# The token gather of a routed mixture-of-experts stage: one fp32 product, or two single-pass products of a high and a low part

## The chip, the cores and the metric

The kernel runs on one core of one Trainium2 chip. The metric is the device time of one execution in microseconds (us), as a median over repeated runs. The profile used below is that of one further execution.

## What is computed

The reference is a stack of twelve stages over 256 tokens of width 1024 in fp32: an S5 and pooling mixer, a stick-breaking attention, two mixture-of-experts (MoE) feed-forward stages, and a second block of convolution, recurrent and latent-attention mixers with dense feed-forwards. The change touches only the two MoE stages:

```python
def grouped_moe(x, router_w, router_bias, w1, w3, w2):
    xt = x.reshape(-1, d)
    scores = jax.nn.sigmoid((xt @ router_w).astype(F32))
    ...                       # best group of four experts, best two experts in it
    gates = jnp.sum(jax.nn.one_hot(idx, N_EXPERTS, dtype=F32) * w[..., None], axis=1)
    h = jax.nn.silu(jnp.einsum('td,edf->etf', xt, w1)) * jnp.einsum('td,edf->etf', xt, w3)
    h = h * gates.T[:, :, None].astype(h.dtype)
    y = jnp.einsum('etf,efd->td', h, w2)
```

Every token uses one group of four experts only, so the kernel sorts the tokens by group and runs each group's experts on its own tokens.

## The kernel before, in words

**Streams.** All weights come from memory as 840 tiles of 128 x 1024 fp32 values (512 KB), through a ring of six buffers `raw`. For each tile ScalarE (ACT) writes the rounded high part `w_hi` (`split_hi`, L265) and VectorE (DVE) the rest `w_lo = raw - w_hi` (`split_lo`, L272), both of type fp32r, which TensorE (PE) multiplies in a single pass. A weight product is three such products: high x high, low x high, high x low (`three_by_token`, L296 to L298, 512 columns; `three`, L289 to L291, 256 columns). The queue of SyncE issues the loads; a buffer is reloaded when DVE has split it. PE has tile n when DVE has written its `w_lo`.

**An MoE stage.** Its order on each engine is written out by hand. `moe_pe` multiplies the router weights (L758, L759), then the eight tiles of a gate projection (`ple gate`), and inside it `ranks_pe`, which counts how many earlier tokens go to the same group. Meanwhile `route_dve` chooses experts and `slots_dve` turns the choice into a one-hot matrix: `slots[p, tt, s]` (2 x 640 columns) is 1 where token `tt*128 + p` sits in slot s (L938). The largest group has two slot tiles of 128 (the first 256 slots), the three other groups one each (the other 384, `REST`).

**The gather.** `gather_pe` starts when the gate projection ends. It forms the gates by slot (L833, 4 columns), turns the one-hot matrix by ten PE transposes (L841), and then gathers the tokens: `x.T @ slots`, for each 128-wide chunk of the 1024 features over the two token tiles. First the 256 slots of the largest group, two chunks to a PSUM bank, banks `Q[0]` to `Q[3]` (L848, 16 products), then the 384 others, one chunk to a bank, the four banks in turn (L856, 16 products). Operands are plain fp32:

```python
last = nc.tensor.matmul(bank(Q[i])[:, c % 2, :], x[:, tt, c * P:(c + 1) * P], slots[:, tt, 0:T], ...)
last = nc.tensor.matmul(b[:, 0:REST], x[:, tt, k * P:(k + 1) * P], slots[:, tt, T:SLOTS], ...)
```

ACT rounds each filled bank to its high part (L808, L811), DVE subtracts it for the low part (L898, L902) and so frees the bank; `before(pe, Q[i])` makes PE wait for that. In ACT's order (`moe_act`) the three copies of the turned matrix (L803) and two weight tiles (L265) stand ahead of L808, in DVE's order (`moe_dve`) two weight tiles (L272) stand ahead of L898.

**The experts.** `experts_pe` follows at once. The four experts of the largest group pass two token tiles over each weight tile, the other twelve one.

Of the kernel before, what the change touches and what calls it, by code (L numbers as in the profile page):

```python
# [8 lines left out]
F32 = mybir.dt.float32  # L9
# [3 lines left out]
ACT = mybir.ActivationFunctionType  # L13
ALU = mybir.AluOpType
# [3 lines left out]
T = 256  # L18
# [126 lines left out]
def build(nc, dram, columns, stages, known):  # L145
    starts, n_tiles = stream_plan(stages)
    ctx = ExitStack()
    with ctx:
# [63 lines left out]
        def region(at, *shape):  # L212

            size = math.prod(shape)
            ap = scr[:, at:at + size]
            if len(shape) == 2:
                return ap.rearrange("p (a b) -> p a b", b=shape[1])
            if len(shape) == 3:
                return ap.rearrange("p (a b c) -> p a b c", b=shape[1], c=shape[2])
            return ap  # L220

        def column(name, i=0, n=1):
            at = columns[name] + i
            return par[:, at:at + n]
# [4 lines left out]
        def bank(b):  # L229
            return b[:, :].rearrange("p (a t) -> p a t", t=T)  # L230
# [13 lines left out]
        x_first = region(9216, KC, T)  # L244
        ple_tanh = region(6144, TT, D)
        routing = region(8704, 512)
        slots = region(9216, TT, SLOTS)
        slots_turned = c_hi[:, 4:4 + SLOT_TILES + 1, :]

        class Stream:  # L250
# [7 lines left out]
        def split_hi(act, tiles=2):  # L258

            for n in range(act_at.tile, min(act_at.tile + tiles, n_tiles)):  # L260
                act.wait_ge(raw_in[n % RING], 16 * (n // RING + 1))
                if n >= RING:
                    used, count = pe_did.tile(n - RING)
                    act.wait_ge(used, count)
                nc.scalar.activation(w_hi[:, n % RING, :], raw[:, n % RING, :], ACT.Copy).then_inc(hi_done, 1)  # L265
                act_at.tile = n + 1

        def split_lo(dve, tiles=2):

            for n in range(dve_at.tile, min(dve_at.tile + tiles, n_tiles)):  # L270
                dve.wait_ge(hi_done, n + 1)
                nc.vector.tensor_tensor(w_lo[:, n % RING, :], raw[:, n % RING, :],  # L272
                                        w_hi[:, n % RING, :].bitcast(F32), ALU.subtract).then_inc(lo_done, 1)
                dve_at.tile = n + 1
# [509 lines left out]
        def moe_act(act, st):  # L784
            def tanh_of_gate(half):
                for tt in range(TT):
                    act.wait_ge(pe_did["ple gate"], pe_did.at("ple gate", st, half, tt))
                    nc.scalar.activation(ple_tanh[:, tt, half_of(half)], Q[2 * half + tt][:, :], ACT.Tanh, scale=0.5).then_inc(
                        act_did["ple tanh"], act_did.next("ple tanh", st, half, tt))

            split_hi(act)
            split_hi(act)
            act.wait_ge(dve_did["logits"], dve_did.at("logits", st))
            nc.scalar.activation(routing[:, 0:32], routing[:, 480:512], ACT.Tanh, scale=0.5).then_inc(
                act_did["router tanh"], act_did.next("router tanh", st))
            split_hi(act)
            tanh_of_gate(0)
            split_hi(act)
            tanh_of_gate(1)
            for i in range(3):  # L800
                act.wait_ge(pe_did["gathered"], pe_did.at("gathered", st, "turned", i))
                n = min(2, SLOT_TILES - 2 * i)
                nc.scalar.activation(slots_turned[:, 2 * i:2 * i + n, :], bank(Q[1 + i])[:, 0:n, :], ACT.Copy).then_inc(  # L803
                    act_did["xg_hi"], act_did.next("xg_hi", st, "turned", i))
            split_hi(act)
            for i in range(4):
                act.wait_ge(pe_did["gathered"], pe_did.at("gathered", st, i))
                nc.scalar.activation(pair(x_hi, i), bank(Q[i]), ACT.Copy).then_inc(act_did["xg_hi"], act_did.next("xg_hi", st, i))  # L808
            for k in range(KC):
                act.wait_ge(pe_did["gathered"], pe_did.at("gathered", st, 4 + k))  # L810
                nc.scalar.activation(xg_hi[:, k, :], Q[k % 4][:, 0:REST], ACT.Copy).then_inc(act_did["xg_hi"], act_did.next("xg_hi", st, 4 + k))  # L811
# [15 lines left out]
        def gather_pe(pe, st):  # L827
            before(pe, Q[0])
            pe.wait_ge(dve_did["slots"], dve_did.at("slots", st))
            gate4 = routing[:, 392:400].rearrange("p (t e) -> p t e", t=TT)  # L830
            for j in range(SLOT_TILES):
                for tt in range(TT):
                    last = nc.tensor.matmul(Q[0][:, 4 * j:4 * j + 4], slots[:, tt, j * P:(j + 1) * P], gate4[:, tt, :],  # L833
                                            start=tt == 0, stop=tt == TT - 1, skip_group_check=True)
            last.then_inc(pe_did["gathered"], pe_did.next("gathered", st, "gates"))
            after(Q[0], ("dve", ("xg_lo", st, "gates")))
            for i in range(3):
                before(pe, Q[1 + i])
                for j in range(2 * i, min(2 * i + 2, SLOT_TILES)):
                    for tt in range(TT):  # L840
                        last = nc.tensor.transpose(bank(Q[1 + i])[:, j % 2, tokens(tt)], slots[:, tt, j * P:(j + 1) * P], column("ident", 0, P))  # L841
                last.then_inc(pe_did["gathered"], pe_did.next("gathered", st, "turned", i))
                after(Q[1 + i], ("act", ("xg_hi", st, "turned", i)))
            for i in range(4):
                before(pe, Q[i])
                for c in (2 * i, 2 * i + 1):
                    for tt in range(TT):
                        last = nc.tensor.matmul(bank(Q[i])[:, c % 2, :], x[:, tt, c * P:(c + 1) * P], slots[:, tt, 0:T],  # L848
                                                start=tt == 0, stop=tt == TT - 1, skip_group_check=True)
                last.then_inc(pe_did["gathered"], pe_did.next("gathered", st, i))  # L850
                after(Q[i], ("dve", ("xg_lo", st, i)))
            for k in range(KC):
                b = Q[k % 4]
                before(pe, b)
                for tt in range(TT):
                    last = nc.tensor.matmul(b[:, 0:REST], x[:, tt, k * P:(k + 1) * P], slots[:, tt, T:SLOTS], start=tt == 0, stop=tt == TT - 1)  # L856
                last.then_inc(pe_did["gathered"], pe_did.next("gathered", st, 4 + k))
                after(b, ("dve", ("xg_lo", st, 4 + k)))

# [23 lines left out]
        def moe_dve(dve, st):  # L883
            split_lo(dve)
            split_lo(dve)
            dve.wait_ge(pe_did["logits"], pe_did.at("logits", st))
            nc.vector.tensor_reduce(routing[:, 480:512], Q[3][:, 0:2 * TT * N_EXPERTS].rearrange("p (t j e) -> p t e j", t=TT, j=2),
                                    AX.X, ALU.add).then_inc(dve_did["logits"], dve_did.next("logits", st))
            route_dve(dve, st)
            slots_dve(dve, st)  # L890
            split_lo(dve)
            split_lo(dve)
            dve.wait_ge(pe_did["gathered"], pe_did.at("gathered", st, "gates"))
            nc.vector.tensor_copy(slot_gate, Q[0][:, 0:4 * SLOT_TILES]).then_inc(dve_did["xg_lo"], dve_did.next("xg_lo", st, "gates"))
            split_lo(dve)
            for i in range(4):
                dve.wait_ge(act_did["xg_hi"], act_did.at("xg_hi", st, i))
                nc.vector.tensor_tensor(pair(x_lo, i), bank(Q[i]), pair(x_hi, i).bitcast(F32), ALU.subtract).then_inc(  # L898
                    dve_did["xg_lo"], dve_did.next("xg_lo", st, i))
            for k in range(KC):  # L900
                dve.wait_ge(act_did["xg_hi"], act_did.at("xg_hi", st, 4 + k))
                nc.vector.tensor_tensor(xg_lo[:, k, :], Q[k % 4][:, 0:REST], xg_hi[:, k, :].bitcast(F32), ALU.subtract).then_inc(  # L902
                    dve_did["xg_lo"], dve_did.next("xg_lo", st, 4 + k))
# [3 lines left out]
        def slots_dve(dve, st):  # L907
# [27 lines left out]
                                      column("tile_base", 0, SLOT_TILES).unsqueeze(1).to_broadcast([P, TT, SLOT_TILES]), ALU.subtract))  # L935
            for tt in range(TT):
                for j in range(SLOT_TILES):
                    last = nc.vector.tensor_scalar(slots[:, tt, j * P:(j + 1) * P], column("iota", 0, P), offset[:, tt, j:j + 1], None, ALU.is_equal)  # L938
            last.then_inc(dve_did["slots"], dve_did.next("slots", st))


# [1738 lines left out]
```

## Time and profile before

| What | Value |
|---|---|
| median of three runs | 2455.26 us (2454.24 to 2455.89) |
| the profiled execution, its own time | 2457.98 us |
| its span in the trace | 2456.2 us |
| PE busy | 2239.3 us, 91% |
| DVE busy | 1585.4 us, 65% |
| ACT busy | 1195.9 us, 49% |
| bytes moved | 452.19 MB, 184 GB/s over the span |
| mean granted TensorE clock | 0.955 of full |

The span is what the trace covers; the execution's own time is 1.8 us longer. Times in the trace count from the span's start. A matmul record lasts from its start to its modelled end, and records overlap, so the cost of one in a dense row of them is the distance between two starts. An fp32 matmul of the program appears as two records, an fp32r one as one.

### The profile page before, as it was taken

To read this page: it belongs to the slowest core of one execution; us is meant where nothing else is said; L and a number is where in the kernel's file an instruction comes from. 1 tells how busy PE (TensorE), PEld (TensorE's weight loads), DVE (VectorE), ACT (ScalarE), POOL (GpSimd) and SP (SyncE) were. 2 spreads that over 40 slices of the span, in tenths; PEclk is the share of its full clock that TensorE was granted. 3 is DMA by queue.
4 is the path that set the end of the run, shared out by engine and by line. 5 is a ranking of instruction groups with operands and counts; after the bars stand their busy time and mean duration, and the time that the engine had idled before them with its cause. 6 is when DMAs were issued, how large, how long until landed. Compare 5 with 4: busy or idle time off the path is not lost.

```text
span 2456.2 us, 29573 instructions
## 1 busy us (share of the span) xinstructions
PE 2239.3 (91%) x11242; PEld 1875.9 (76%) x11242; DVE 1585.4 (65%) x2080; ACT 1195.9 (49%) x1485; POOL 40.0 (2%) x41
## 2 busy tenths in 40 slices
PE   5479999997999999999899998699985899999999
PEld 5257887776977888787798887588874688888887
DVE  7975557888436556888765548755557555566554
ACT  3124446775453445777435444654443354444443
POOL 1220000000000000000000000000000000000000
PEclk9688999998998999999899999799997899999999
DMA  6023558997502456999555553355541155545653
GB/s 246 18 77 113 196 191 302 341 349 273 193 31 94 156 196 225 335 353 350 171 190 180 184 188 130 103 182 195 188 139 52 42 181 190 187 157 173 203 190 102
DMA packets 123165, 452.19 MB, mean 184 GB/s; under 512 B 13808, under 2 KB 13808, under 8 KB 122128
## 3 DMA queue, kind: packets, MB, share of 16 engines
q1 hardware_dynamic: 121680, 442.55, 52.6%
q0 software_dynamic: 1056, 6.95, 0.8%
q8 instruction: 90, 1.47, 0.2%
q10 hardware_dynamic: 288, 0.80, 0.1%
q14 instruction: 51, 0.42, 0.0%
HBM read 449.19 MB, written 1.05 MB: 183 GB/s over the span
## 4 chain that ended last, share of the span: by engine, by line
PE 78%; DVE 13%; ACT 3%; DMA 3%; issue 2%; POOL 1%; SPq 0%; ACTq 0%; DVEq 0%; POOLq 0%
PE bank L296 19%; PE bank L297 19%; PE bank L298 19%; DVE w_lo L272 4%; PE bank L289 4%; PE bank L290 4%; PE bank L291 4%; DMA raw<-in_stream 2%; ACT w_hi L265 1%; PE bank L856 1%; DVE scr L2242 1%; PE bank L581 1%; DVE scr L2226 1%; PE bank L848 1%; DVE scr L1611 1%
## 5 line engine op out<-in xcount | busy, mean ns | idle before, releaser
L272 DVE TENSOR_TENSOR w_lo<-raw,w_hi 128x1024 fp32r<-128x1024 f32 x840 | 1003.1, 1223 | 533.5 <-ACT w_hi L265 530.1
L265 ACT ACTIVATE w_hi<-raw 128x1024 fp32r<-128x1024 f32 x840 | 875.1, 1058 | 729.5 <-PE bank L298 547.8
L296 PE MATMUL bank<-w_hi,x_hi 128*128 128x512 f32 x1024 | 404.1, 395 | 4.8 <-DVE x_lo L491 4.8
L297 PE MATMUL bank<-w_lo,x_hi 128*128 128x512 f32 x1024 | 400.5, 391 | 0.0
L298 PE MATMUL bank<-w_hi,x_lo 128*128 128x512 f32 x1024 | 400.4, 391 | 0.0
L296 PE MATMUL bank<-w_hi,c_hi 128*128 128x512 f32 x872 | 344.2, 395 | 42.8 <-issue 21.1
L297 PE MATMUL bank<-w_lo,c_hi 128*128 128x512 f32 x872 | 342.0, 392 | 0.0
L298 PE MATMUL bank<-w_hi,c_lo 128*128 128x512 f32 x872 | 341.8, 392 | 0.0
L289 PE MATMUL bank<-x_hi,w_hi 128*128 128x256 f32 x792 | 228.1, 288 | 25.6 <-DVE w_lo L272 20.9
L296 PEld LDWEIGHTS bank<-w_hi,x_hi 128*128 128x128 f32 x1024 | 193.6, 189 | 45.2 <-issue 5.6
L296 PEld LDWEIGHTS bank<-w_hi,c_hi 128*128 128x128 f32 x872 | 165.2, 189 | 80.7 <-issue 46.4
L290 PE MATMUL bank<-x_lo,w_hi 128*128 128x256 f32 x792 | 226.6, 286 | 0.0
L291 PE MATMUL bank<-x_hi,w_lo 128*128 128x256 f32 x792 | 226.4, 286 | 0.0
L298 PEld LDWEIGHTS bank<-w_hi,x_lo 128*128 128x128 f32 x1024 | 193.4, 189 | 40.7
L297 PEld LDWEIGHTS bank<-w_lo,x_hi 128*128 128x128 f32 x1024 | 193.5, 189 | 39.4
L298 PEld LDWEIGHTS bank<-w_hi,c_lo 128*128 128x128 f32 x872 | 165.3, 190 | 35.2
L297 PEld LDWEIGHTS bank<-w_lo,c_hi 128*128 128x128 f32 x872 | 165.4, 190 | 34.0
L289 PEld LDWEIGHTS bank<-x_hi,w_hi 128*128 128x128 f32 x792 | 154.8, 195 | 27.0 <-issue 20.8
L296 PE MATMUL bank<-w_hi,xg_hi 128*128 128x512 f32 x384 | 154.9, 403 | 6.4 <-DVE c_lo L1147 5.9
L290 PEld LDWEIGHTS bank<-x_lo,w_hi 128*128 128x128 f32 x792 | 154.8, 195 | 0.0
L291 PEld LDWEIGHTS bank<-x_hi,w_lo 128*128 128x128 f32 x792 | 154.6, 195 | 0.0
L297 PE MATMUL bank<-w_lo,xg_hi 128*128 128x512 f32 x384 | 151.6, 395 | 0.0
(391 smaller groups left out, 2236.8 us busy)
## 6 DMA issues: line engine op xcount, KB each, us to landing
raw<-in_stream SPq DMA_DIRECT2D x840, 512.0 KB, 4.3
ln_rows<-in_ln POOLq DMA_DIRECT2D x4, 1024.0 KB, 4.9
scr<-in_xt SPq DMA_DIRECT2D x1, 1024.0 KB, 5.2
scr<-in_s POOLq DMA_DIRECT2D x1, 1024.0 KB, 12.2
x<-in_x POOLq DMA_DIRECT2D x1, 1024.0 KB, 17.0
out_x<-x SPq DMA_DIRECT2D x4, 256.0 KB, 2.8
par<-in_par ACTq DMA_DIRECT2D x1, 752.5 KB, 9.2
scr<-in_ple POOLq DMA_DIRECT2D x1, 512.0 KB, 9.3
```

Of the source, the lines that this page charges most:

```text
L265: nc.scalar.activation(w_hi[:, n % RING, :], raw[:, n % RING, :], ACT.Copy).then_inc(hi_done, 1)
L272: nc.vector.tensor_tensor(w_lo[:, n % RING, :], raw[:, n % RING, :], w_hi[:, n % RING, :].bitcast(F32), ALU.subtract).then_inc(lo_done, 1)
L289: nc.tensor.matmul(out, hi, xh, start=start, stop=False, skip_group_check=shared)
L290: nc.tensor.matmul(out, hi, xl, start=False, stop=False, skip_group_check=shared)
L291: return nc.tensor.matmul(out, lo, xh, start=False, stop=stop, skip_group_check=shared)
L296: nc.tensor.matmul(out, xh, hi, start=start, stop=False)
L297: nc.tensor.matmul(out, xh, lo, start=False, stop=False)
L298: return nc.tensor.matmul(out, xl, hi, start=False, stop=stop)
L581: mm = nc.tensor.transpose(bank(H3[j])[:, c % 2, tokens(tt)], hidden[:, tt, c * P:(c + 1) * P], column("ident", 0, P))
L848: last = nc.tensor.matmul(bank(Q[i])[:, c % 2, :], x[:, tt, c * P:(c + 1) * P], slots[:, tt, 0:T], start=tt == 0, stop=tt == TT - 1, skip_ ...
L856: last = nc.tensor.matmul(b[:, 0:REST], x[:, tt, k * P:(k + 1) * P], slots[:, tt, T:SLOTS], start=tt == 0, stop=tt == TT - 1)
L1611: last = nc.vector.scalar_tensor_tensor(dst, src, w, dst, ALU.mult, ALU.add)
```

## The change

The one-hot matrix is now written as fp32r into a part of `c_lo` that is free at that time; the gates (L833 before) and the transposes (L841 before) read the same bits as fp32. ACT copies the token rows `x` to a rounded high part `x_rows_hi` (in the memory of `y_hi`), two instructions of 128 x 1024 behind the router's tanh. DVE subtracts it, `x_rows_lo` (in the memory of `y_lo`), two instructions between the first and second pair of weight tiles behind `slots_dve`. Each fp32 product of the gather becomes two fp32r products, one with each part, into the same accumulation. PE waits once per token tile for `x_rows_lo`.

```diff
-        slots = region(9216, TT, SLOTS)
+        slots_r = c_lo[:, 4:9, :].rearrange("p a t -> p (a t)").rearrange("p (t s) -> p t s", t=TT)
+        slots = slots_r.bitcast(F32)
+        x_rows_hi, x_rows_lo = (ap[:, :, :].rearrange("p a b -> p (a b)").rearrange("p (t d) -> p t d", t=TT) for ap in (y_hi, y_lo))
...
             nc.scalar.activation(routing[:, 0:32], routing[:, 480:512], ACT.Tanh, scale=0.5).then_inc(
                 act_did["router tanh"], act_did.next("router tanh", st))
+            for tt in range(TT):
+                nc.scalar.activation(x_rows_hi[:, tt, :], x[:, tt, :], ACT.Copy).then_inc(act_did["x_hi"], act_did.next("x_hi", st, "rows", tt))
             split_hi(act)
...
                     for tt in range(TT):
-                        last = nc.tensor.matmul(bank(Q[i])[:, c % 2, :], x[:, tt, c * P:(c + 1) * P], slots[:, tt, 0:T],
-                                                start=tt == 0, stop=tt == TT - 1, skip_group_check=True)
+                        if i == 0:
+                            pe.wait_ge(dve_did["x_lo"], dve_did.at("x_lo", st, "rows", tt))
+                        for part in (x_rows_hi, x_rows_lo):
+                            last = nc.tensor.matmul(bank(Q[i])[:, c % 2, :], part[:, tt, c * P:(c + 1) * P], slots_r[:, tt, 0:T],
+                                                    start=tt == 0 and part is x_rows_hi, stop=tt == TT - 1 and part is x_rows_lo,
+                                                    skip_group_check=True)
...
                 for tt in range(TT):
-                    last = nc.tensor.matmul(b[:, 0:REST], x[:, tt, k * P:(k + 1) * P], slots[:, tt, T:SLOTS], start=tt == 0, stop=tt == TT - 1)
+                    for part in (x_rows_hi, x_rows_lo):
+                        last = nc.tensor.matmul(b[:, 0:REST], part[:, tt, k * P:(k + 1) * P], slots_r[:, tt, T:SLOTS],
+                                                start=tt == 0 and part is x_rows_hi, stop=tt == TT - 1 and part is x_rows_lo)
...
             slots_dve(dve, st)
             split_lo(dve)
+            for tt in range(TT):
+                dve.wait_ge(act_did["x_hi"], act_did.at("x_hi", st, "rows", tt))
+                nc.vector.tensor_tensor(x_rows_lo[:, tt, :], x[:, tt, :], x_rows_hi[:, tt, :].bitcast(F32), ALU.subtract).then_inc(
+                    dve_did["x_lo"], dve_did.next("x_lo", st, "rows", tt))
             split_lo(dve)
...
-                    last = nc.vector.tensor_scalar(slots[:, tt, j * P:(j + 1) * P], column("iota", 0, P), offset[:, tt, j:j + 1], None, ALU.is_equal)
+                    last = nc.vector.tensor_scalar(slots_r[:, tt, j * P:(j + 1) * P], column("iota", 0, P), offset[:, tt, j:j + 1], None, ALU.is_equal)
```

On DVE, from the one-hot matrix to the low parts of the gathered tokens, the order before (`bank` is PSUM, `scr` the scratch memory in which `slots` lay):

```order
L934 TENSOR_TENSOR scr<-scr,par 128x10
L938 TENSOR_SCALAR scr<-par,scr 128x128 x10
L272 TENSOR_TENSOR w_lo<-raw,w_hi 128x1024 x4
L894 COPY norm<-bank 128x20
L272 TENSOR_TENSOR w_lo<-raw,w_hi 128x1024 x2
L898 TENSOR_TENSOR x_lo<-bank,x_hi 128x512 x4
L902 TENSOR_TENSOR xg_lo<-bank,xg_hi 128x384 x8
```

and with the change:

```order
L948 TENSOR_TENSOR scr<-scr,par 128x10
L952 TENSOR_SCALAR c_lo<-par,scr 128x128 x10
L274 TENSOR_TENSOR w_lo<-raw,w_hi 128x1024 x2
L904 TENSOR_TENSOR y_lo<-x,y_hi 128x1024 x2
L274 TENSOR_TENSOR w_lo<-raw,w_hi 128x1024 x2
L908 COPY norm<-bank 128x20
L274 TENSOR_TENSOR w_lo<-raw,w_hi 128x1024 x2
L912 TENSOR_TENSOR x_lo<-bank,x_hi 128x512 x4
L916 TENSOR_TENSOR xg_lo<-bank,xg_hi 128x384 x8
```

The two subtractions of the token rows split the run of four weight tiles in two; behind them the order is as it was.

On PE, the gather before, from the last product of the gate projection:

```order
L298 MATMUL bank<-w_hi,x_lo 128x512
L833 MATMUL bank<-scr 128x4 x10
L841 MATMUL bank<-par,scr 128x128 x10
L848 MATMUL bank<-scr,x 128x256 x16
L856 MATMUL bank<-scr,x 128x384 x16
```

and with the change, up to the second pair of the 32 products of 256 columns (the 32 of 384 columns are L865 and alternate in the same way):

```order
L300 MATMUL bank<-w_hi,x_lo 128x512
L837 MATMUL bank<-scr,c_lo 128x4 x10
L845 MATMUL bank<-par,c_lo 128x128 x10
L855 MATMUL bank<-c_lo,y_hi 128x256
L855 MATMUL bank<-c_lo,y_lo 128x256
```

The gates and transposes keep their place; each product of the gather is now a pair, with `y_hi` and `y_lo` holding the parts of the token rows.

## Rows read from the trace of the kernel before

**Rows 1.** The chain of waits that ended last: shares by engine.

```profile
PE 78%; DVE 13%; ACT 3%; DMA 3%; issue 2%; POOL 1%; SPq 0%; ACTq 0%; DVEq 0%; POOLq 0%
```

**Rows 2.** Timeline of PE, first MoE stage: start, length, line, count, idle before.

```profile
218.92 2.29 PE L833 MATMUL bank<-scr 128*128 128x4 f32 x20
...
222.20 7.07 PE L848 MATMUL bank<-scr,x 128*128 128x256 f32 x32
229.11 10.48 PE L856 MATMUL bank<-scr,x 128*128 128x384 f32 x32
...
239.66 0.39 PE L297 MATMUL bank<-w_lo,x_hi 128*128 128x512 f32 x1
```

**Rows 3.** The same, second MoE stage.

```profile
809.13 7.07 PE L848 MATMUL bank<-scr,x 128*128 128x256 f32 x32
816.04 10.48 PE L856 MATMUL bank<-scr,x 128*128 128x384 f32 x32
```

**Rows 4.** Timeline of PE: single-pass products, of 256 columns, then of 512.

```profile
617.80 0.28 PE L290 MATMUL bank<-x_lo,w_hi 128*128 128x256 f32 x1
...
618.88 0.28 PE L290 MATMUL bank<-x_lo,w_hi 128*128 128x256 f32 x1
...
243.78 0.39 PE L297 MATMUL bank<-w_lo,x_hi 128*128 128x512 f32 x1
...
244.91 0.39 PE L296 MATMUL bank<-w_hi,x_hi 128*128 128x512 f32 x1
```

**Rows 5.** Groups by shape, 193 to 241 us: busy us, mean ns, idle before.

```profile
L265 ACT ACTIVATE w_hi<-raw 128x1024 fp32r<-128x1024 f32 x8 | 8.3, 1060 | 7.5 <-PE bank L298 6.4 <-DMA raw<-in_stream 1.1
L272 DVE TENSOR_TENSOR w_lo<-raw,w_hi 128x1024 fp32r<-128x1024 f32 x6 | 7.2, 1220 | 4.1 <-ACT w_hi L265 4.1
```

**Rows 6.** Timeline of ACT, first MoE stage.

```profile
198.96 1.06 ACT L265 ACTIVATE w_hi<-raw 128x1024 fp32r<-128x1024 f32 x1 [4.73 <-PE bank L298]
...
222.98 2.01 ACT L265 ACTIVATE w_hi<-raw 128x1024 fp32r<-128x1024 f32 x2
224.87 0.61 ACT L808 ACTIVATE x_hi<-bank 128x512 fp32r<-128x512 f32 x1
...
230.60 0.49 ACT L811 ACTIVATE xg_hi<-bank 128x384 fp32r<-128x384 f32 x1 [0.69 <-PE bank L856]
```

**Rows 7.** Timeline of DVE, first MoE stage.

```profile
207.02 2.35 DVE L272 TENSOR_TENSOR w_lo<-raw,w_hi 128x1024 fp32r<-128x1024 f32 x2
...
221.25 0.18 DVE L894 COPY norm<-bank 128x20 f32<-128x20 f32 x1 [7.93 <-PE bank L833]
224.08 2.36 DVE L272 TENSOR_TENSOR w_lo<-raw,w_hi 128x1024 fp32r<-128x1024 f32 x2 [2.65 <-ACT w_hi L265]
226.35 1.28 DVE L898 TENSOR_TENSOR x_lo<-bank,x_hi 128x512 fp32r<-128x512 f32 x2
...
231.12 0.56 DVE L902 TENSOR_TENSOR xg_lo<-bank,xg_hi 128x384 fp32r<-128x384 f32 x1 [0.49 <-ACT xg_hi L811]
```

**Rows 8.** Two waits of PE, and stretches: length, busy by engine, PEclk, DMA, GB/s.

```profile
159.54 0.47 PE L296 MATMUL bank<-w_hi,c_hi 128*128 128x512 f32 x1 [2.11 <-DVE c_lo L2314]
...
174.65 0.50 PE L296 MATMUL bank<-w_hi,p_hi 128*128 128x512 f32 x1 [0.96 <-DVE x L452]
...
161.20:164.50 3.30, 3.30 (x10) 2.52 (x9) 3.30 (x4) 2.99 (x4) 0.00 (x0) 0.52 0.49 159
...
170.00:180.00 10.00, 8.32 (x38) 6.31 (x37) 9.23 (x20) 1.51 (x5) 0.00 (x0) 1.00 0.37 147
187.00:190.00 3.00, 3.00 (x16) 3.00 (x15) 3.00 (x3) 2.98 (x4) 0.00 (x0) 0.50 0.41 164
...
218.70:222.00 3.30, 3.30 (x31) 3.26 (x30) 0.18 (x1) 0.85 (x2) 0.00 (x0) 1.00 0.01 2
```

**Rows 9.** The supply of weights: a stretch in the two-pass experts; waits in the single-pass ones.

```profile
250.00:260.00 10.00, 10.00 (x46) 8.29 (x45) 4.81 (x4) 5.35 (x6) 0.00 (x0) 1.00 0.69 214
...
ACT w_hi L265 <- DMA raw<-in_stream: 15.5, 30, 1.6
```

## The prediction

> **What bounds the kernel now.** I read the chain of waits first: 78% of it is PE and 13% DVE [rows 1], so work taken off PE counts where PE runs without a gap. The timeline of PE tells whether the gather is such a place [rows 2]: the gates start at 218.92 us, the gather's first part (L848) at 222.20, its second (L856) at 229.11, and no row of it has idle time before it. The second product of the experts starts at 239.66; one spacing of 512 columns (0.23 us, below) ahead of it stands the first, at 239.43. So the gather proper takes 6.91 + 10.32 = 17.23 us, all of it PE. The second MoE stage shows the same, 6.91 us between its two parts [rows 3]. Two stages hold 34.5 us of gather, 1.4% of the time; nothing else is touched.
>
> **The cost of the products.** Before, 16 products of 256 columns take 6.91 us, 0.432 us each, and 16 of 384 take 10.32 us, 0.645 us each. After, there are 32 and 32 single-pass ones. Single-pass products of 256 columns, each with its own load of a 128 x 128 operand as here, stand nine apart in 618.88 - 617.80 = 1.08 us, which is 0.120 us each; those of 512 columns stand five apart in 1.13 us, 0.226 us each [rows 4]. For 384 columns no row exists. The bounds are these two, 0.120 and 0.226; I take the middle, 0.173, since 384 is the middle of 256 and 512 and a time made of a fixed part and one per column is straight between them. The first part then takes 32 x 0.120 = 3.84 us and the second 32 x 0.173 = 5.54 us, 9.38 together: 7.85 us less per stage.
>
> The Trainium skill (TensorE: Matmul & The Clock Gate, Back-to-back issue gap) gives another price for loads and products in a sustained stream, about 81 ns at 128 columns and 131 ns at 512; the trace contradicts it at 512 columns (226 ns), and by it the gather would be bound by DVE and the total about 1.5 us lower than I forecast, as an estimate.
>
> **What becomes late.** PE now empties its work faster than the banks are drained. The first part would end at 222.20 + 3.84 = 226.04. The second begins in `Q[0]`, which is free when DVE has done the first L898. That stands behind two weight tiles of DVE that start at 224.08, when ACT's own two tiles (from 222.98) have given the first, and it starts at 226.35 [rows 6, 7]. None of this depends on the gather: ACT's tiles follow the copies of the turned matrix, and ACT is ready for the first bank at 224.87 without idle time [rows 6]. One L898 takes 0.69 us (two take 1.28, so a spacing of 0.59) [rows 7], and `Q[0]` is free at 227.04; with some 0.06 us for the signal PE goes on at 227.1. That is a new wait of 1.06 us per stage. Behind it are all the rest of the gather and the experts, so it counts in full.
>
> After that the banks come in time. DVE frees `Q[1]` to `Q[3]` every 0.59 us, at 227.6, 228.2 and 228.8, and PE needs 4 x 0.173 = 0.69 us for each. The second round of a bank needs PE 0.69, ACT 0.49 and DVE 0.56 us [rows 6, 7] with the signals between them about 2 us, against 4 x 0.69 = 2.8 us in which PE returns to it. So the second part ends at 227.1 + 5.54 = 232.64 instead of 239.43: **6.79 us less per stage, 13.6 us in all.** The bounds: with no wait 7.85 per stage, 15.7; with 0.226 us for 384 columns the second part takes 7.23 us, 5.1 per stage, 10.2; with 0.120 us DVE binds, twelve subtractions of about 0.59 and 0.5 us from 226.35 put the end near 231.4, 8.0 per stage, 16.1.
>
> **What is added.** ACT: two copies of 128 x 1024, 1.06 us each [rows 5], behind the router's tanh. ACT idles 4.73 us there until 198.96 [rows 6]; 2.1 us fit. Were they to wait there longer than that, the next weight tiles would be late. DVE: two subtractions of 128 x 1024, 1.22 us each [rows 5], 2.4 us, from 207.02 + 2.35 = 209.4 to 211.7. They push the next two weight tiles by 0.9 us or so; DVE then idles 7.93 us until 221.25 [rows 7], and PE reads those tiles only behind the gather. The rows' low part is there 10 us before PE asks. Both cost nothing; without that cover DVE's would cost at most 2.4 us per stage. The one-hot matrix is written by the same ten DVE instructions as before; an fp32r output costs L272 nothing that shows, so I take no change. Gates and transposes keep type and place.
>
> **The sum.** 2 x 6.79 = 13.6 us off the profiled execution's own 2457.98 (span 2456.2) gives 2444.4. That execution is 2.7 us above the median; against the median 2455.26 it is **2441.7 us**.
>
> **The rivals.** A measurement of this kernel can tell about 0.2%, 4.9 us, from no change.
>
> (A) *The clock falls in the new wait.* PE waited 2.11 us ahead of 159.54 and then had 0.52 of full clock (its level of 1.2 GHz) over 161.2 to 164.5, in the middle of dense products; ahead of 174.65 it waited 0.96 us and the stretch around it shows 1.00 [rows 8]. The new wait of 1.06 us is near the harmless one, but it comes 4 us behind 3.3 us of thin work (gates and transposes). That thin stretch itself shows 1.00 [rows 8]. A low stretch of 3.3 us costs half its length, 1.65 us per stage: 2441.7 + 3.3 = 2445.0 us. The Trainium skill (TensorE: Matmul & The Clock Gate, Part 4: PE-mode transpose) says that transposes do not count as work for the clock; the trace does not show it harming here, with 1.00 granted over the ten transposes, but by that rule the wait would follow a longer idle stretch and (A) would be what happens.
>
> (B) *The change does not do what it says*: a product with these operands, written by ACT and DVE into borrowed memory, costs PE what a record of the fp32 product costs now (0.216 and 0.322 us, half of a product each). There are 64 such records before and 64 products after, so nothing is gained: 2455.3 us. Against it: L289 to L291 have operands of the same type and shape at 0.120 us [rows 4].
>
> (C) *The gain is given back to the weight stream.* The single-pass experts wait 15.5 us in 30 pieces for loads [rows 9]. Had the stream run without pause from before the gather until there, arriving earlier would only lengthen these waits: 2455.3 us. Against it: in the two-pass experts PE is busy 10.00 of 10.00 us at 214 GB/s [rows 9], so loads wait for PE there for some 130 us, and the ring is full at their end however early they began.
>
> (D) *Slower: the clock falls in the new wait and stays low.* Place: the wait ahead of `Q[0]`. Each microsecond at the low level costs 0.5 us; it decides from 2 x 6.79 = 13.6 us of low clock per stage. Low clock over the rest of the gather (5.5 us) and the first expert's eight tiles (96 products of 0.226, 21.8 us) would cost 13.7 us per stage: 2441.7 + 27.3 = 2469.0 us. For it: at the router the clock stood at 0.50 [rows 8] under thin products. Against it: here dense products follow, and behind 159.54 they had full clock again after 164.5.
>
> **How the numbers follow.** Forecast 0.84, (A) 0.07, (B) 0.03, (C) 0.04, (D) 0.02. The forecast's bounds are 2455.3 - 16.1 = 2439.2 and 2455.3 - 10.2 = 2445.1; with (A) at 2445.0 and about 1 us of scatter in a median the range is 2438.6 to 2446.6, which leaves out (B), (C), (D) and a little of the rest. Faster by over 0.2% are the forecast and (A), 0.91; within it (B) and (C), 0.07; slower (D), 0.02.
>
> **What would show it.** Right: 64 products per stage, 0.120 and about 0.173 us apart; one wait of PE of about 1 us ahead of the first product of 384 columns, released by DVE's L912; experts from about 232.7 us; DVE's idle ahead of L908 shorter by 2.4 us at no cost; clock 1.00 over the gather. Wrong: records of 0.2 us or more apart at 256 columns (B); a PEclk near 0.5 between 226 and 240 (A, D); the gather shorter by 6.8 us but the end of the stage not earlier, with more waits for loads (C); several waits for banks in the second part, if DVE's or ACT's spacing is larger than the rows say.

## The result, and the profile after

| | before | after |
|---|---|---|
| median, measured side by side | 2455.75 us (2454.24 to 2461.28, 6 runs) | 2444.22 us (2440.93 to 2444.77, 6 runs) |
| ratio after/before | | 0.9944, 95% interval 0.9934 to 0.9954 |
| the profiled execution, its own time | 2457.98 us | 2444.77 us |
| its span | 2456.2 us | 2442.1 us |
| PE busy | 2239.3 us | 2223.9 us |

The changed kernel is faster by 0.56%, 13.7 us by the ratio. The forecast, 2441.7 us, is 0.9945 of the median on which it was made, inside the interval. As an absolute time it is 2.5 us too low (2444.22 us), and rival (A)'s 2445.0 us is nearer, so the time alone doesn't choose between the two; the traces below do. The two medians are 11.5 us apart and the two spans 14.1 us, so a single figure is good to about 2 us.

The page of the changed kernel, the busy time of its engines (us, share of the span, instructions) and the shares of its chain of waits:

```profile
PE 2223.9 (91%) x11242; PEld 1871.2 (77%) x11242; DVE 1589.6 (65%) x2084; ACT 1199.7 (49%) x1489; POOL 40.0 (2%) x41
...
PE 78%; DVE 13%; ACT 3%; issue 2%; DMA 2%; POOL 1%; SPq 0%; ACTq 0%; DVEq 0%; POOLq 0%
```

PE lost 15.4 us of busy time, DVE and ACT gained 4.2 and 3.8 us for four subtractions and four copies, and the chain is PE's as before [rows 1].

The timeline of PE in the changed kernel's second MoE stage (start us, length us, line and operation, count, in brackets the idle time before and its releaser), to be held against [rows 3]:

```profile
798.56 2.29 PE L837 MATMUL bank<-scr,c_lo 128*128 128x4 f32 x20
...
801.75 0.36 PE L855 MATMUL bank<-c_lo,y_hi 128*128 128x256 f32 x1
...
805.40 0.28 PE L855 MATMUL bank<-c_lo,y_hi 128*128 128x256 f32 x1
805.52 0.28 PE L855 MATMUL bank<-c_lo,y_lo 128*128 128x256 f32 x1
...
806.73 0.44 PE L865 MATMUL bank<-c_lo,y_hi 128*128 128x384 f32 x1 [0.93 <-DVE x_lo L912]
807.01 0.34 PE L865 MATMUL bank<-c_lo,y_lo 128*128 128x384 f32 x1
...
811.94 0.34 PE L865 MATMUL bank<-c_lo,y_lo 128*128 128x384 f32 x1
...
812.47 0.40 PE L298 MATMUL bank<-w_hi,x_hi 128*128 128x512 f32 x1
```

The reader is to see three things. Products of 256 columns are 0.12 us apart (805.40 and 805.52). Exactly one wait has appeared, 0.93 us, ahead of the first product of 384 columns and released by L912. From the second of these products to the thirtieth are 811.94 - 807.01 = 4.93 us over 28 spacings, 0.176 us each. From the first gate product to the experts it takes 812.47 - 798.56 = 13.91 us. Before, it took 239.43 - 218.92 = 20.51 us [rows 2], and the second stage had the same.

The same view of the first stage, to be held against [rows 2]:

```profile
218.54 2.29 PE L837 MATMUL bank<-scr,c_lo 128*128 128x4 f32 x20
220.69 1.29 PE L845 MATMUL bank<-par,c_lo 128*128 128x128 f32 x10
221.73 0.36 PE L855 MATMUL bank<-c_lo,y_hi 128*128 128x256 f32 x1
...
222.27 0.41 PE L855 MATMUL bank<-c_lo,y_lo 128*128 128x256 f32 x1
222.49 0.41 PE L855 MATMUL bank<-c_lo,y_hi 128*128 128x256 f32 x1
...
225.46 0.28 PE L855 MATMUL bank<-c_lo,y_hi 128*128 128x256 f32 x1
...
227.12 0.34 PE L865 MATMUL bank<-c_lo,y_hi 128*128 128x384 f32 x1
...
232.75 0.39 PE L298 MATMUL bank<-w_hi,x_hi 128*128 128x512 f32 x1
```

Here no wait is shown, and from 222.27 the products stand some 0.21 us apart. The windows of this stage say why (length, busy us of PE, PEld, DVE, ACT and POOL, PEclk, DMA share, GB/s):

```profile
218.70:222.00 3.30, 3.30 (x32) 3.30 (x32) 0.18 (x1) 1.24 (x3) 0.00 (x0) 1.00 0.00 0
222.00:225.40 3.40, 3.40 (x18) 3.40 (x18) 1.71 (x2) 3.20 (x6) 0.00 (x0) 0.50 0.00 0
225.40:232.70 7.30, 7.30 (x48) 7.30 (x47) 6.39 (x11) 5.09 (x10) 0.00 (x0) 1.00 0.41 144
```

For 3.4 us TensorE ran at the lower of its two levels, 1.2 GHz, from 0.3 us into the gather on, behind the gates and transposes and before any wait for a bank. The stage took 232.75 - 218.54 = 14.21 us, only 0.30 us more than the other: the slow products used up the time in which PE would have waited for `Q[0]`. The two stages thus gave 6.3 and 6.6 us, 12.9 together. The first also began 0.4 us earlier.

What was added, in the timeline of ACT, then that of DVE, both of the changed kernel's first stage:

```profile
193.79 1.99 ACT L799 ACTIVATE y_hi<-x 128x1024 fp32r<-128x1024 f32 x2
...
198.58 1.06 ACT L267 ACTIVATE w_hi<-raw 128x1024 fp32r<-128x1024 f32 x1 [2.81 <-PE bank L300]
```

```profile
208.91 2.36 DVE L904 TENSOR_TENSOR y_lo<-x,y_hi 128x1024 fp32r<-128x1024 f32 x2
...
220.86 0.18 DVE L908 COPY norm<-bank 128x20 f32<-128x20 f32 x1 [7.33 <-PE bank L837]
```

The next weight tile of ACT starts at 198.58, with 2.81 us of idle time still ahead of it where there were 4.73 [rows 6]. DVE's copy of the gates also waits for PE, 7.33 us after 7.93 [rows 7]. That is only 0.60 us less, though 2.4 us of work were added. The next pair of weight tiles starts at 211.18 here; before, idle time stood ahead of it, and the subtractions took its place:

```profile
210.84 2.48 DVE L272 TENSOR_TENSOR w_lo<-raw,w_hi 128x1024 fp32r<-128x1024 f32 x2 [1.47 <-ACT w_hi L265]
```

The supply of the single-pass experts did not change either (waits over 370 to 590 us of the changed kernel: total, times, longest), against 15.5 us in 30 pieces before [rows 9]:

```profile
ACT w_hi L267 <- DMA raw<-in_stream: 15.2, 33, 1.4
```

### The profile page after: what moved, and what is told of

Its sections match the earlier page's. It is cut to its first block, busy times and chain, and to the rows that moved or that the text cites. A ratio compares the mean times of both kernels' runs of the same rounds, so it can differ in the third digit from the quotient of the medians.

```text
span 2442.1 us, 29583 instructions
## 1 busy us (share of the span) xinstructions
PE 2223.9 (91%) x11242; PEld 1871.2 (77%) x11242; DVE 1589.6 (65%) x2084; ACT 1199.7 (49%) x1489; POOL 40.0 (2%) x41
## 4 chain that ended last, share of the span: by engine, by line
PE 78%; DVE 13%; ACT 3%; issue 2%; DMA 2%; POOL 1%; SPq 0%; ACTq 0%; DVEq 0%; POOLq 0%
PE bank L298 20%; PE bank L300 19%; PE bank L299 19%; DVE w_lo L274 4%; PE bank L291 4%; PE bank L292 4%; PE bank L293 4%; DMA raw<-in_stream 2%; ACT w_hi L267 1%; DVE scr L2256 1%; PE bank L583 1%; DVE scr L2240 1%; PE bank L1017 1%; DVE scr L1625 1%; PE bank L2066 0%
```

## The experiments

Two questions were open. Is the gain made of the parts that the forecast named? And what lowered the clock, which the forecast had put, as a rival, into the new wait? Two theories stood for the second: T, that the thin work ahead (gates and transposes) does it in some executions, and S, that the single-pass products with their short wait do. "Stage time" below is from the first gate product to the first product of the experts: 20.51 us before, 14.21 and 13.91 us in the changed kernel. Lines of edits are shown against the changed kernel unless said otherwise.

**The changed kernel again.** No edit.

> The changed kernel again. Measured so far: the first stage's gather spent 222.0 to 225.4 us at half clock (1.7 us lost, the expected wait for Q[0] hidden in it), the second stage had no such stretch and a wait of 0.93 us. Theory T (thin work): the clock falls because the gates and the transposes, 3.3 us of little streaming, stand ahead of the gather, and whether it does varies from execution to execution: another profile shows it in the first stage, the second, both or neither, and the times of the executions spread over some 3 us. Theory S (single pass): the single-pass products hold the clock less well than the fp32 ones; then a low stretch lies inside the products, in both stages, in most profiles. Both: 11.5 to 14 us below the kernel before.

2442.55 us, ratio 0.9941 (0.9928 to 0.9954). Stage times 14.34 and 13.91 us. The first had the low clock again, this time already in the transposes (window 220 to 222 us at 0.50), the second had 1.00 and a wait of 0.93 us. A fall that starts before the gather's first single-pass product speaks against S.

**First part in fp32 again.** The 256-column products as before, the 384-column ones as changed.

```diff
-                        for part in (x_rows_hi, x_rows_lo):
-                            last = nc.tensor.matmul(bank(Q[i])[:, c % 2, :], part[:, tt, c * P:(c + 1) * P], slots_r[:, tt, 0:T], ...
+                        last = nc.tensor.matmul(bank(Q[i])[:, c % 2, :], x[:, tt, c * P:(c + 1) * P], slots[:, tt, 0:T], ...
```

> The first part of the gather (16 products of 256 columns) is fp32 again, the second single-pass. Additive theory: the second part gives 10.32 - 5.6 = 4.7 us per stage with no wait for a bank, since the first part now ends behind DVE's first bank; 9.4 us in all below the kernel before, some 3 us above the changed one. If the wait for Q[0] or the clock ate the first part's gain, this would be equal to the changed kernel or faster. Theory S expects a low stretch in the second part; theory T at most one at the start of the fp32 part.

2447.68 us, ratio 0.9957 (0.9944 to 0.9969). The first stage took 15.81 us, 4.70 less than before: the second part alone. The fp32 part and a window of its second stage:

```profile
802.74 8.72 PE L854 MATMUL bank<-c_lo,x 128*128 128x256 f32 x32
```

```profile
802.70:806.00 3.30, 3.30 (x10) 2.68 (x9) 1.42 (x2) 2.79 (x5) 0.00 (x0) 0.50 0.01 2
```

The fp32 products themselves fell to the low clock, 8.72 us for the 7.07 of [rows 3]: 1.65 us lost where nothing waits. S does not explain this.

**The split of a pair moved behind the gather.** DVE is late for `Q[0]` because two weight tiles stand ahead of L912. Here this pair is split behind the last of the gather's twelve banks, on both engines (ACT's place is shown, DVE's is the same).

```diff
-            split_hi(act)
             for i in range(4):
                 act.wait_ge(pe_did["gathered"], pe_did.at("gathered", st, i))
...
                 act.wait_ge(pe_did["gathered"], pe_did.at("gathered", st, 4 + k))
                 nc.scalar.activation(xg_hi[:, k, :], Q[k % 4][:, 0:REST], ACT.Copy).then_inc(act_did["xg_hi"], act_did.next("xg_hi", st, 4 + k))
+            split_hi(act)
```

> The changed kernel with the pair of weight tiles (ACT and DVE) that stood ahead of the first gathered bank moved behind the last one. Theory of the wait: PE's wait ahead of the first product of 384 columns goes from 0.93 us to none, and where the clock does not fall the gather ends 0.9 us sooner, so 1 to 2 us below the changed kernel in all. Rival: the pair comes too late for the experts (needed 5.4 us behind the gather's end, ready some 3.5 us behind it) and a wait of PE for w_lo appears in the first expert; then equal or slower.

2440.68 us, ratio 0.9931 (0.9919 to 0.9942). Timeline of PE and window of its second stage:

```profile
797.84 2.29 PE L837 MATMUL bank<-scr,c_lo 128*128 128x4 f32 x20
...
804.80 0.28 PE L855 MATMUL bank<-c_lo,y_lo 128*128 128x256 f32 x1
804.91 0.34 PE L865 MATMUL bank<-c_lo,y_hi 128*128 128x384 f32 x1
...
810.54 0.40 PE L298 MATMUL bank<-w_hi,x_hi 128*128 128x512 f32 x1
```

```profile
797.80:810.50 12.70, 12.70 (x95) 12.66 (x94) 6.20 (x11) 7.77 (x15) 0.00 (x0) 1.00 0.01 1
```

The wait is gone and the stage takes 12.70 us, 1.21 less than 13.91: the wait counted in full, as forecast, and its cause was the pair. The rival, that the pair now comes too late for the experts, did not come: PE shows no wait in the two-pass experts behind either gather. The first stage fell to the low clock (14.25 us) and gained nothing, since there the slow products had covered the wait. With no wait left to cover it, the fall costs 14.25 - 12.70 = 1.55 us.

**The gates in the gate projection.** The gate products are split off and stand together behind the sixth of the projection's eight tiles; only the transposes are left ahead of the gather.

```diff
+                    if half == 1 and part == 1:
+                        gates_pe(pe, st)
```

> The changed kernel with the gates by slot (ten fp32 products of 4 columns, 2.1 us) moved into the gate projection, between its second and third tile of the second half. Same work on PE. Theory T: only the transposes (1.15 us) are left ahead of the gather, the clock stays at 1.00 in it in both stages, and the time is 0 to 2 us below the changed kernel. Theory S: a stretch near 0.5 still shows inside the gather's products, time as the changed kernel. A fall might instead follow the gates inside the projection, which would cost as much as before.

2442.53 us, ratio 0.9937 (0.9924 to 0.995). Windows of its first stage, the gates (they start at 213.49), what follows them in the projection, and the transposes with the gather:

```profile
213.40:215.70 2.30, 2.30 (x23) 2.26 (x21) 0.53 (x1) 0.00 (x0) 0.00 (x0) 1.00 0.97 381
215.70:219.00 3.30, 3.30 (x9) 2.62 (x9) 0.18 (x1) 0.00 (x0) 0.00 (x0) 0.50 0.68 262
222.70:234.50 11.80, 10.89 (x76) 10.55 (x74) 8.00 (x12) 9.09 (x17) 0.00 (x0) 1.00 0.28 89
```

The fall went with the gates: it hit the projection's products of 512 columns, and the gather ran at 1.00 with waits of 0.91 us in both stages. The second stage shows 1.00 throughout, so the moved gates brought a fall in one stage of two. The ten transposes alone left the clock at 1.00.

**The gates spread in twos, and the pair behind.** Each slot tile's two gate products stand behind another group of the projection's products.

```diff
+                        if half == 1 and 0 <= 2 * part + tt - 2 < SLOT_TILES:
+                            gates_pe(pe, st, 2 * part + tt - 2)
```

> The kernel with the weight pair behind the gather, and the ten products of the gates spread in five twos over the second half of the gate projection, each two behind six dense products of 512 columns. So far a low stretch of 3.4 us followed the gates in 4 of 10 stages of this kernel and its variants, also where the gather's first part was fp32 and also where the gates stood together inside the projection: theory T (the thin work, not the single pass). T expects here 1.00 from 200 us to the end of the first gather and the same in the second stage, the gather from its transposes to the first expert in 10.6 us in both, and a time 1 to 3 us below that of the pair alone. If low stretches still show, the transposes or the single-pass products are the cause, and the time is that of the pair alone.

2438.59 us, ratio 0.9929 (0.9914 to 0.9944), the fastest of all. Windows from the projection to the experts, first and second stage:

```profile
200.00:231.50 31.50, 31.50 (x183) 28.22 (x182) 18.69 (x48) 12.61 (x21) 0.00 (x0) 1.00 0.36 134
790.00:811.30 21.30, 21.30 (x132) 19.59 (x131) 9.62 (x15) 9.28 (x17) 0.00 (x0) 1.00 0.36 146
```

No gap of PE and no low clock in either; from the first transpose to the experts 10.55 and 10.60 us.

**Products of the high part only.** The low part's products are left out, so this kernel gathers the tokens without their low bits. It asks where DVE becomes the bound.

```diff
-                        for part in (x_rows_hi, x_rows_lo):
+                        for part in (x_rows_hi,):
```

> The changed kernel without the products of the low part: 16 + 16 single-pass products per stage. It leaves out the low part of the gathered tokens. Theory of the bound: PE's work falls by another 1.9 + 2.8 = 4.7 us per stage, but the wait for Q[0] grows to about 3 us (DVE's first subtraction still starts some 7.5 us behind the gates) and then DVE's twelve subtractions bind, so the gather from gates to first expert takes 12.4 to 12.8 us instead of 13.9: only 1.1 to 1.5 us per stage less, 2 to 3 in all. Rival (PE is still the bound of the gather): 9 us in all.

2439.23 us, ratio 0.993 (0.9911 to 0.9949). Its second stage, PE and then DVE:

```profile
797.70 2.29 PE L837 MATMUL bank<-scr,c_lo 128*128 128x4 f32 x20
...
800.90 2.14 PE L855 MATMUL bank<-c_lo,y_hi 128*128 128x256 f32 x16
...
805.88 4.27 PE L865 MATMUL bank<-c_lo,y_hi 128*128 128x384 f32 x16 [2.84 <-DVE x_lo L912]
810.04 0.47 PE L298 MATMUL bank<-w_hi,x_hi 128*128 128x512 f32 x1
```

```profile
805.14 2.48 DVE L912 TENSOR_TENSOR x_lo<-bank,x_hi 128x512 fp32r<-128x512 f32 x4
807.53 3.80 DVE L916 TENSOR_TENSOR xg_lo<-bank,xg_hi 128x384 fp32r<-128x384 f32 x8
```

Half of the products are gone, but this stage takes 12.34 us, 1.57 less than 13.91. DVE's twelve subtractions now follow each other without a pause, and PE waits 2.84 us for the first of them: with the pair in its old place this is the floor, however cheap products get. The first stage took 13.35 us. It had the usual low stretch, from 221.1 us, and then a second one, which began 1.1 us behind a wait for the bank:

```profile
226.78 5.09 PE L865 MATMUL bank<-c_lo,y_hi 128*128 128x384 f32 x16 [1.53 <-DVE x_lo L912]
```

```profile
227.90:231.30 3.40, 3.40 (x11) 3.23 (x11) 3.14 (x7) 2.35 (x6) 0.00 (x0) 0.51 0.44 152
```

This is the fall that rival (A) describes, behind a wait of 1.53 us; in the second stage none followed one of 2.84 us.

**Copies and subtractions twice.** The added work of ACT and DVE is done a second time, with the same values.

```diff
+            for again in range(2):
...
+            for again in range(2):
```

> The changed kernel with ACT's two copies and DVE's two subtractions of the token rows done twice. Prediction's claim: both lie in idle time (ACT 4.7 us long, of which 2.0 used; DVE 7.3 us left), so doubling costs nothing on DVE and nothing or a few tenths on ACT (4.0 of 4.7 us); time as the changed kernel. Rival: they delay the next weight tiles; then up to 2 us per stage more.

2444.26 us, ratio 0.995 (0.9937 to 0.9964). Timelines of ACT and DVE in its first stage:

```profile
193.58 4.17 ACT L802 ACTIVATE y_hi<-x 128x1024 fp32r<-128x1024 f32 x4
197.65 1.04 ACT L267 ACTIVATE w_hi<-raw 128x1024 fp32r<-128x1024 f32 x1
```

```profile
207.92 4.87 DVE L910 TENSOR_TENSOR y_lo<-x,y_hi 128x1024 fp32r<-128x1024 f32 x4
...
219.87 0.18 DVE L914 COPY norm<-bank 128x20 f32<-128x20 f32 x1 [4.81 <-PE bank L840]
```

Doubled, ACT's copies fill its idle time to the end, DVE keeps 4.81 us, and the gathers take 14.27 and 13.90 us as without doubling. In the second stage ACT's copies start 24.74 us ahead of the gates, and 24.92 us in the changed kernel, so nothing between them became longer. The added work is hidden.

**The kernel before, with its gates twice.** The edit is on the kernel before: thin work longer, all products fp32.

```diff
-            for j in range(SLOT_TILES):
+            for j in [*range(SLOT_TILES), *range(SLOT_TILES)]:
```

> The kernel before (fp32 gather) with the ten products of the gates done twice: 4.3 us of thin products and 1.15 us of transposes ahead of the gather. Theory T: now the clock falls in both stages although every product of the gather is fp32, with a low stretch of 3.4 us or more near the gather's start; cost 2 x (2.15 + 1.7) = 7.7 us. Theory S (only single-pass products lose the clock): 1.00 throughout, cost 4.3 us.

2466.95 us, ratio 1.0044 (1.0029 to 1.0058). PE in its first stage, then windows of the first and the second:

```profile
217.64 6.11 PE L833 MATMUL bank<-scr 128*128 128x4 f32 x40
223.61 2.38 PE L841 MATMUL bank<-par,scr 128*128 128x128 f32 x10
225.78 7.74 PE L848 MATMUL bank<-scr,x 128*128 128x256 f32 x32
```

```profile
220.50:227.00 6.50, 6.50 (x29) 6.29 (x29) 0.18 (x1) 2.00 (x4) 0.00 (x0) 0.50 0.00 0
812.00:818.00 6.00, 6.00 (x22) 5.31 (x22) 2.19 (x3) 3.47 (x6) 0.00 (x0) 0.53 0.00 0
```

Both stages fell, with no single-pass product in the gather, so S is out. The cost is 10.8 us by the ratio (7.1 to 14.3 by its interval). S's 4.3 us lies outside, T's 7.7 us near the lower end. The traces decide: the stages took 26.04 and 26.07 us, 5.5 us more than 20.51 each, where T gave 3.85. The low stretch lasts some 6.8 us per stage, twice that of the other kernels. T had its place right and its length wrong.

**Gates spread, the pair in its old place.**

> The changed kernel with the gates spread over the gate projection, the weight pair in its old place. It tells the two gains of the last version apart. Expected: clock 1.00 in both gathers, the wait for Q[0] of 0.9 us back in both stages (up to 1.1, since it is hidden by nothing now), transposes to first expert 11.5 us; the time 0.5 to 1.5 us below the changed kernel and some 1.9 us above the version with both. If the pair's place is worth nothing, both are equal.

2444.24 us, ratio 0.9953 (0.994 to 0.9967). 1.00 over both gathers, and both now show the wait (0.96 and 0.92 us). From the first transpose to the experts 11.79 and 11.78 us, 1.2 more than with the pair behind. Without a fall the wait is paid in both stages, so the spreading alone gains next to nothing: in the changed kernel the same piece took 12.06 us in the fallen stage and 11.77 us in the other. The interval of the ratio overlaps that of the changed kernel.

**The kernel before, once more.**

> The kernel before once more, for a second profile. Theory T: its gates and transposes take 3.3 us too, so a low stretch of 3.4 us can appear in one of its two stages (none did in the first profile, 1 of 2 in the variant whose first part is fp32); seen or not, from the gates' start to the first expert 20.5 us without, 22.2 with one.

A profile of 2457.32 us. The timeline of PE in its first stage:

```profile
217.98 2.29 PE L833 MATMUL bank<-scr 128*128 128x4 f32 x20
220.13 1.86 PE L841 MATMUL bank<-par,scr 128*128 128x128 f32 x10
221.79 8.21 PE L848 MATMUL bank<-scr,x 128*128 128x256 f32 x32
229.84 10.48 PE L856 MATMUL bank<-scr,x 128*128 128x384 f32 x32
```

The unchanged kernel falls too: transposes 1.86 us, first part 8.21 us (7.07 in [rows 2]), the second part its old 10.48 us, and the stage 22.18 us, 1.67 more than 20.51. The profile of before on which the forecast was made happened to show no fall.

**The pair behind, and both, again.** Two repeats beside each other on one chip.

> The weight pair behind the gather once more: no wait for Q[0] in either stage, gates to first expert 12.7 us where the clock holds and 14.3 where it falls; 15 to 18 us below the kernel before.

> Pair behind the gather and gates spread, once more, beside the others on one chip: clock 1.00 in both gathers, transposes to first expert 10.6 us in both, no wait; 1 to 3 us below the pair alone, 16 to 20 below the kernel before. If it is equal to the pair alone, the saved low stretches are lost elsewhere, or below what the spread of single executions lets be seen.

The pair alone: 2440.56 us, ratio 0.9941 (0.9928 to 0.9955), stage times 14.28 (low clock) and 12.71 us. With the gates spread: 2440.66 us, ratio 0.9938 (0.9924 to 0.9951), clock 1.00 in both stages, 10.60 and 10.55 us behind the first transpose. Both beat the kernel before. All four runs of these two versions have medians 1.9 to 5.6 us under those of the changed kernel (2442.55 and 2444.22 us), and the traces show 1.2 us per unfallen stage. But the intervals of the ratios overlap with the changed kernel's, and the medians of the kernel before, measured beside these runs, themselves lie between 2455.19 and 2458.38 us. So the times alone don't show the gain over the changed kernel, and between the two versions no difference can be told.

## Why the prediction was right

**The products.** 256 columns: 0.120 us forecast and measured. 384 columns: 0.173 forecast as the middle of [rows 4], 0.176 measured, so the straight line between 256 and 512 columns held. The Trainium skill (TensorE: Matmul & The Clock Gate, Back-to-back issue gap) gives about 131 ns per product for sustained streams of 512 columns. The trace does not agree: already at 384 columns products come 176 ns apart. As the prediction estimates, DVE would bind the gather at such a price; only the kernel with half of the products showed that. The "about 1.5 us" beside it is a slip: the prediction's own bound with DVE binding, 16.1 us of gain, is 2.5 us below its forecast. Measured, that floor lay 1.57 us under 13.91 in the stage that kept its clock, 3.1 us for two.

**The wait.** 1.06 us forecast ahead of `Q[0]`, 0.93 measured in the stage whose clock held, at the place and by the releaser named; moving the pair took it away and gave 1.21 us. The forecast's steps from the first gate product on: up to the gather 3.28 us, 3.19 measured; first part and wait 4.90 us, 4.98 measured; second part 5.54 us, 5.74 measured, of which 0.10 is its spacing and the rest that the first product behind the wait takes 0.28 us. Together 13.91 for 13.72: the gain of this stage was 6.6 us where 6.79 was forecast. The other stage gave 6.3 us by another path: its products were slow and it had no wait. That the sum came out there too is partly luck, since the two nearly replace each other.

**The cover.** ACT's copies and DVE's subtractions cost nothing, and not even their double did. One sign was read wrong: DVE's idle time ahead of L908 was to be 2.4 us shorter and was 0.60, because most of the subtractions went into the 1.47 us of idle time that stood ahead of the next pair. The prediction's own 0.9 us by which the pair is pushed already contradicted the 2.4.

**The rivals.** (B), no gain in the products, and (C), the gain given back to the loads, are refuted by the rows above. (D), slower by a clock that stays low, did not come: behind the low stretch full clock returned inside the gather. Its price was also too small by half: 21.8 us is what the 96 products take at full clock, so losing the clock over them and the 5.5 us of gather would add the same 27.3 us again in each stage, not 13.7. (A) was half right. A low stretch of about the length forecast is there, but in the changed kernel not behind the new wait: it comes ahead of it, in the kernel before as well, and behind no idle time. Seven waits of 0.91 to 0.96 us for the bank stand in the traces of all versions, and no fall follows any of them. Of the two longer ones, both in the kernel with half of the products, one (1.53 us) had a fall behind it and one (2.84 us) had none, so (A)'s mechanism is not ruled out for longer waits. What failed is the step "that thin stretch itself shows 1.00": it was read from one execution, and in the next one of the same kernel it does not hold. The price failed too. The 1.65 us held for fp32 products (8.72 for 7.07 us), and nearly for single-pass ones where no wait was left (1.55 us), but in the changed kernel the fall cost 0.30 us, since it took the place of the bank wait.

**The clock.** With the ten gate products of usual count right ahead of the gather there are nine profiles, 18 stages: the clock fell in 8 of them, seven times in the first stage and once in the second, at 0.88 to 0.90 on average over the stretch from 213 to 228 or 795 to 812 us. With the gates spread it fell in none of 6 stages, with doubled gates in both of 2, and where the gates were moved, in 1 of 2, and the fall moved with them. Each of these eleven falls began 2.2 to 3.7 us behind the first gate product. By place and count it is shown that the thin products bring the fall on, though the counts are small; why one execution falls and the next doesn't stays open, and so does why the first stage falls more often. The Trainium skill (TensorE: Matmul & The Clock Gate, Part 4: PE-mode transpose) says that transposes don't count as work for the clock; the traces neither show nor exclude it: ten transposes without the gates right ahead of them left the clock at 1.00 in all 6 spread stages and both with the gates moved. The moved gates, with no transpose near, brought a fall by themselves.

**Not settled.** Single executions differ by some us in stretches that no edit touched: from the first expert behind the first gather to the gates of the second stage it took 563.4 to 568.5 us in the ten profiles with the gates ahead of the gather. So the 12.9 us of both gathers and the 13.7 us of the ratio cannot be told apart, and that the ratio meets the 13.6 us of the forecast to 0.1 us is partly luck.

## What to carry to other kernels

When products get cheaper, ask at once what drains their banks: here the time gained uncovered one wait, made by two weight tiles that stood ahead of the drain, and moving one pair behind it took the wait away. Read the clock of a place from several executions, because a fall that comes in one of two makes a single profile say either thing. And a wait and a slow stretch in front of it hide each other, so the gain of removing one alone can be nothing: spreading the gates without moving the pair gave next to none.

## What the runs showed of the hardware

- Twenty records of 4 columns and ten transposes, 3.2 us in which the profile calls PE busy throughout, were followed by a stretch of about 3.4 us at 1.2 GHz in 8 of 18 stages, with no idle time ahead. Doubling the gate products made it some 6.8 us, in both stages.
- Single-pass products of 384 columns with a load each: 0.176 us apart at full clock. Products of 256 columns: 0.120 us, and 0.21 us at the low level, 1.8 times as much.
- A product of 384 columns that restarts PE behind a wait is dearer than one in a stream: 0.28 us to the next one instead of 0.176.
- Seven waits of PE for `Q[0]` of 0.91 to 0.96 us, with the 256-column products ahead and the 384-column ones behind, were followed by no low stretch; of two longer ones, 1.53 us was and 2.84 us was not.
